# Streaming expert weights on one Trainium2 core: handing over whole 1024-column blocks in place of halves

## The reference

```python
def peer_ffn(h, w_q, sub_keys, expert_u, expert_v):
    ...
    v1, i1 = lax.top_k(s1, PEER_TOPK)
    v2, i2 = lax.top_k(s2, PEER_TOPK)
    cand = (v1[..., :, None] + v2[..., None, :]).reshape(t, PEER_HEADS, PEER_TOPK * PEER_TOPK)
    cs, ci = lax.top_k(cand, PEER_TOPK)
    ...
    gates = jax.nn.softmax(cs, axis=-1)
    def mix(args):
        hc, ec, gc = args
        a = jax.nn.gelu(jnp.einsum('chkd,cd->chk', expert_u[ec], hc).astype(jnp.float32))
        w = (gc * a).astype(hc.dtype)
        return jnp.einsum('chk,chkd->cd', w, expert_v[ec])
```

## Time and profile before

| | us |
|---|---|
| median of 3 executions (3075.44 to 3093.64) | 3091.76 |
| the profiled execution | 3091.76 |
| its span, first to last instruction | 3089.8 |
| TensorE busy in the span | 3043.7 |
| VectorE busy | 2096.0 |
| ScalarE busy | 1603.9 |
| `w_u` stage, from about 789 to 1521 us of the span | 732 |
| `w_v` stage, from 1522 to about 2242 us | 720 |

### The profile page before, as it was taken

How to read it: one execution, slowest core, us unless ns; L and a number is a source line. 1 busy time by engine, 2 the same in 40 slices (tenths; PEclk the granted TensorE clock), 3 DMA queues, 4 the chain that set the end, 5 groups by cost and what they waited for, 6 DMA issues and landing times.

```text
span 3089.8 us, 45798 instructions
## 1 busy us (share of the span) xinstructions
PE 3043.7 (99%) x14773; PEld 2514.2 (81%) x14773; DVE 2096.0 (68%) x4127; ACT 1603.9 (52%) x2955; POOL 480.4 (16%) x341
## 2 busy tenths in 40 slices
PE   7999999999999999999999999999999999999998
PEld 6888787788888888888888888888878888877787
DVE  4567677656888888766666666666576676568864
ACT  4445464455555555555555555555564445546553
POOL 1000000000087867770000000000000000000000
PEclk9999999999999999999999999999999999999999
DMA  6777554466577777886766666666666555653355
GB/s 225 252 256 238 174 159 150 152 189 201 177 190 185 187 188 186 188 185 191 235 209 214 207 214 206 214 227 202 185 190 194 167 177 177 197 170 119 112 157 166
DMA packets 197197, 588.00 MB, mean 190 GB/s; under 512 B 54608, under 2 KB 54736, under 8 KB 195776
## 3 DMA queue, kind: packets, MB, share of 16 engines
q1 hardware_dynamic: 148688, 537.99, 55.8%
q0 software_dynamic: 48368, 48.20, 7.9%
HBM read 565.00 MB, written 21.10 MB: 190 GB/s over the span
## 4 chain that ended last, share of the span: by engine, by line
PE 96%; DVE 2%; DMA 1%; ACT 1%; issue 0%; SPq 0%; POOL 0%; DVEq 0%; ACTq 0%
PE bank L814 17%; PE bank L589 14%; PE bank L591 13%; PE bank L590 13%; PE bank L815 9%; PE bank L884 8%; PE bank L886 8%; PE bank L885 8%; PE bank L654 2%; PE bank L559 1%; PE bank L666 1%; DVE lo L1464 1%; DMA raw<-in_w_narrow 0%; PE bank L677 0%; PE bank L676 0%; DMA raw<-in_w_att 0%
## 5 line engine op out<-in xcount | busy, mean ns | idle before, releaser
L1047 ACT ACTIVATE hi<-raw 128x512 fp32r<-128x512 f32 (+1 forms) x2042 | 1284.7, 632 | 1367.3 <-PE bank L591 640.6
L1464 DVE TENSOR_TENSOR lo<-raw,hi 128x512 fp32r<-128x512 f32 (+1 forms) x2042 | 1388.9, 692 | 843.1 <-ACT hi L1047 826.1
L814 PE MATMUL bank<-xt,hi 128*128 128x512 f32 x2304 | 813.6, 398 | 0.1
L589 PE MATMUL bank<-hi,xt 128*128 128x512 f32 (+1 forms) x1924 | 768.2, 399 | 14.5 <-DVE lo L1464 14.3
L591 PE MATMUL bank<-hi,xt 128*128 128x512 f32 (+1 forms) x1924 | 751.2, 390 | 0.0
L590 PE MATMUL bank<-lo,xt 128*128 128x512 f32 (+1 forms) x1924 | 749.7, 390 | 0.0
L815 PE MATMUL bank<-xt,lo 128*128 128x256 f32 x2304 | 646.5, 281 | 0.0
L814 PEld LDWEIGHTS bank<-xt,hi 128*128 128x128 f32 x2304 | 432.8, 188 | 107.3 <-issue 0.4
L435 POOL DMA_INDIRECT gates_scratch<-picked,place x256 | 420.3, 1642 | 269.2 <-DVE picked L1961 161.4
L589 PEld LDWEIGHTS bank<-hi,xt 128*128 128x128 f32 x1924 | 363.7, 189 | 97.6 <-issue 21.7
L815 PEld LDWEIGHTS bank<-xt,lo 128*128 128x128 f32 x2304 | 435.1, 189 | 0.0
(11 more groups left out here) (215 smaller groups left out, 1598.7 us busy)
## 6 DMA issues: line engine op xcount, KB each, us to landing
raw<-in_w_u SPq DMA_DIRECT2D x256, 512.0 KB
raw<-in_w_v SPq DMA_DIRECT2D x256, 512.0 KB
raw<-in_w_ein SPq DMA_DIRECT2D x128, 512.0 KB
raw<-in_w_oin SPq DMA_DIRECT2D x72, 512.0 KB
raw<-in_w_att SPq DMA_DIRECT2D x64, 512.0 KB
raw<-in_w_gate SPq DMA_DIRECT2D x64, 512.0 KB
gates_scratch<-u_low POOLq DMA_DIRECT2D x16, 1024.0 KB, 7.5
raw<-in_w_out SPq DMA_DIRECT2D x32, 512.0 KB
```

The costliest lines, as they stand in the source:

```text
L589: pe.matmul(acc, xh, h_[:, s], start=first, stop=False)
L814: pe.matmul(acc[:, :], h_[:, s], xt[:, tile].rearrange("p w t -> p (w t)"), start=first, stop=False)
L1047: act.activation(hi[d][:, c], raw[s][:, c], ACT.Copy).then_inc(hi_ready, 2 // parts)
L1464: dve.tensor_tensor(lo[d][:, c], raw[s][:, c], hi[d][:, c].bitcast(F32), ALU.subtract)\
```

## The change

In the two expert stages every split is made with `parts=1`: one ScalarE and one VectorE instruction of 1024 columns in place of two of 512. That covers blocks 1 to 255 of `w_u`, all 256 of `w_v` and the first of `w_ein`. TensorE waits once for a block, ahead of its first matmul, and releases it once, by 2, with its last matmul. In `expert_v` the two inner loops change places: token tile `t` outside, half `n` inside. All other stages keep halves. The number of matmuls and their operands stay as they were.

```diff
@@ expert_u
                 for q in range(2):
                     b = FIRST["w_u"] + 2 * j + q
+                    pe.wait_ge(lo_ready, 2 * (b + 1) if i is None else i * 8 + 2 * (b + 1))
                     h_, l_ = hi[b % 2], lo[b % 2]
                     for kk in range(8):
-                        if kk % 4 == 0:
-                            there = 2 * b + kk // 4 + 1
-                            pe.wait_ge(lo_ready, there if i is None else i * 8 + there)
                         k = 8 * q + kk
                         s = slice(kk * P, kk * P + P)
                         mm = weights_by_tokens(bank[6 + g % 2], h_, l_, s, k, k == 0, k == 15)
-                        if kk % 4 == 3:
-                            mm.then_inc(block_used, 1)
+                    mm.then_inc(block_used, 2)
@@ expert_v
-                    if q == 0:
-                        pe.wait_ge(wlo_ready, j + 1 if i is None else i * 2 + (j + 1))
+                    if i is None:
+                        pe.wait_ge(wlo_ready, j + 1)
+                        pe.wait_ge(lo_ready, 2 * (b + 1))
+                    else:
+                        if q == 0:
+                            pe.wait_ge(wlo_ready, i * 2 + (j + 1))
+                        pe.wait_ge(lo_ready, i * 8 + 2 * (b + 1))
                     h_, l_ = hi[b % 2], lo[b % 2]
-                    for n in range(2):
-                        there = 2 * b + n + 1
-                        pe.wait_ge(lo_ready, there if i is None else i * 8 + there)
-                        if first and q == 1 and n == 0:
+                    for t in range(2):
+                        if first and q == 1 and t == 0:
                             pe.wait_ge(added, N_EXPERT_TILES)
-                        for t in range(2):
-                            wh, wl = w_hi[j % 2][:, t * P:t * P + P], w_lo[j % 2][:, t * P:t * P + P]
+                        wh, wl = w_hi[j % 2][:, t * P:t * P + P], w_lo[j % 2][:, t * P:t * P + P]
+                        for n in range(2):
                             acc = bank[4 * t + 2 * q + n][:, :]
...
-                        mm.then_inc(block_used, 1)
+                    mm.then_inc(block_used, 2)
@@ ScalarE, tile_u (both splits; split_v likewise)
-                split(b, i, 4)
+                split(b, i, 4, parts=1)
@@ VectorE, all splits of the two stages
-                split(FIRST["w_u"] + 1 + b)
+                split(FIRST["w_u"] + 1 + b, parts=1)
...
-                split(b)
+                split(b, parts=1)
```

More of the change, by code:

```diff
@@ L1306, in tile_u @@
                     take_low(j - 1, i)
-                split(b + 1, i, 4)
+                split(b + 1, i, 4, parts=1)
                 if i is None:
@@ L1332, in split_v @@
                 b = FIRST["w_v"] + 2 * j + 1
-                split(b, i, 4 if i is not None else 0)
+                split(b, i, 4 if i is not None else 0, parts=1)
                 if i is not None or j + 1 < N_EXPERT_TILES:
                     high_weights(j + 1, i)
-                split(b + 1, i, 4 if i is not None else 0)
+                split(b + 1, i, 4 if i is not None else 0, parts=1)
             take_low(N_EXPERT_TILES - 1)
@@ L2013, in _ @@
                 for n in range(4):
-                    split(FIRST["w_u"] + 1 + 2 * ROUTE_TILES + n, i, 4)
+                    split(FIRST["w_u"] + 1 + 2 * ROUTE_TILES + n, i, 4, parts=1)
                     if n % 2 == 0:
@@ L2049, in _ @@
                     add_x2(1)
-                split(b + 1)
+                split(b + 1, parts=1)
             def ret_take(h):
```

## The result

The changed kernel took 3106.6 us (median of 9 executions, 3101.93 to 3108.12); the kernel before, on the same chip, 3090.91 us (9 executions). The ratio is 1.0054, with a 95% interval of 1.0041 to 1.0067: 0.5% slower, or 15.7 us. The forecast was 3098 us, in a range from 3078 to 3114. The direction held, and most of the mechanism. The size did not: 6 us were expected on top. The working itself reached only to 3105 us, with the long end of every link; 3106.6 lies in the range because it had been widened for the spread of the executions and for the rivals.

The account below looks back on a forecast made before the run. The prediction took TensorE's own pace to bound both expert stages. It added 5 us of stalls in `w_u` and 1 us at the start of `w_v` to 3091.76 us, giving 3098 us, range 3078 to 3114.

Parts of the forecast that it names:

- What bounds it, and what the change gives: Expert stages: TensorE sets the pace; VectorE saves 84 us and ScalarE 108 us of busy time, worth nothing on the path.
- The lead: Expert-stage handover: lead falls from 2.5 us; next block ready at M + 2.65, wanted at 2.82 or 2.80.
- The stalls in `w_u`: Places where VectorE's other work outlasts the lead and TensorE waits: 4.8 us, called 5, with ends 3 and 11.
- the first Exp: In `w_u`, table load, Exp and four picks make VectorE late by 1.06 us; 0.8 us of it new.
- The nine top-16 stretches: In `w_u`, `add_u` with top-16 steps between two splits: 0.1 us over for each of nine, 0.9 us.
- The six with picks: In `w_u`, `add_u` with four picks between two splits: 0.40 us over for each of six, 2.4 us.
- The budget of 1.77: In `w_u`, VectorE's other work between one block's `lo` and the next may take 1.77 us without stalling TensorE.
- The start of `w_v`: Block 1 late by 0.6 us, later weight loads 0.4 us: 1 us in sum, 0.6 to 2.1.
- the first: Rival: a block's chain exceeds its period, so every block in `w_u` and `w_v` pays; 36 us, 3134 us in all; 7%.
- The clock: Rival: each of 17 stalls brings a stretch at half clock on TensorE, 21 us, 3119 us in all; 3%.
- No change: Rival: the stalls do not show, as VectorE's stretches shrink or the lead grows back; 3092 us; 17%.
- faster: Rival: fewer waits and releases on TensorE save 0.06 us a pair, 31 us, giving 3061 us; 4%.

Follow-up runs that it names:

- `splits_whole`: Changed kernel, but TensorE waits for and releases halves and `expert_v` keeps its old loop order; only the splits are whole: 3104.81 us, ratio 1.0054 to the kernel before.
- `one_count_again`: Changed kernel with the three handover semaphores rising by 1, not 2, per whole block in the expert stages, second timing: 3100.34 us, ratio 1.0040 to the kernel before.
- `one_count_even`: Changed kernel with semaphores rising by 1 per whole block and 14 long routing steps per head pair moved to slots without `add_u`: 3104.08 us, ratio 1.0043.
- `even_before`: Kernel before, with 14 long routing steps per head pair, from the second pair on, moved to slots without `add_u`: 3084.07 us, ratio 0.9981.
- `release_whole`: Kernel before with only TensorE's part of the change (waits, releases, loop order); ScalarE and VectorE split by halves: 3089.07 us, ratio 1.0006.
- `scalar_whole`: Kernel before with only ScalarE's splits whole in the expert stages; VectorE's splits and TensorE's waits and releases stay halves: 3089.61 us, ratio 1.0013.

## Why the prediction was right, and where it was off

- **What bounds it, and what the change gives.** Right. TensorE's pace is what it was, VectorE is busy for 71.6 us less (2096.0 to 2024.4; 84 forecast) and ScalarE for 102.5 us less (108 forecast), and none of it reaches the time. The two durations taken from other lines, 1.219 and 1.053 us, came out at 1.227 and 1.061. That TensorE's waits, releases and loop order are worth nothing on the path is borne out by `splits_whole`, which lacks them and is as slow.
- **The lead.** Right in kind. The step that failed is the pair of handovers in it, "M + 0.20" and "0.03 later". Both were read from halves of `w_v`, whose instructions carry the wait that held them. Whole splits had 0.26 and 0.10, the chain 2.80 us in place of 2.65, and VectorE 1.6 us between two blocks in place of 1.77. The prediction named that end (0.26 and 0.11, 11 us) and did not choose it; while routing even that was short, with 0.28, 0.13 and a chain of 2.85. `w_narrow`, whose splits already raised by 2, had it in the trace of before, and so had ScalarE's halves while routing; I looked at durations of long instructions there and not at their starts.
- **The stalls in `w_u`.** 4.8 forecast, 13.9 measured. Of the 9.1 us between them, 6.3 are the "other" blocks, which the prediction put at nothing. Only 1.6 of the 6.3 lie where VectorE's other work reaches up to the split. In the rest of them VectorE was not late but waiting. Two terms were missing there: the chain, read in `w_v` and taken to fit everywhere, was too long beside the routing, and each late start costs 0.07 us on top of its wait. (The prediction saw such a surplus at the first Exp, 0.26 us lost for a wait of 0.15, and did not carry it over.) By `one_count_again` 4.4 of the 6.3 are the handovers' doing. The nine top-16 stretches were mis-sized by themselves: 0.22 us each even with short handovers, in place of 0.1. The six with picks cost 0.55 in place of 0.40. Their durations were read rightly: in `one_count_again` the gap between the splits of the first of them is 907.99 - 905.78 = 2.21 us. The budget of 1.77 was too wide for the routing: there ScalarE starts 0.10 behind TensorE (M + 0.26) in 159 of 160 waits even in `one_count_again`, as its split carries the wait for the load there and not the one for TensorE, and the splits are 0.01 longer each. That makes 1.69, and 2.21 - 1.69 = 0.52 by it. In the trace of before half of the waits in that stretch had this 0.10; the prediction's row came from `w_v`, where all but a few have 0.04.
- **The start of `w_v`.** 1 us forecast, 1.0 measured. Block 1 lost 0.64 us by its start, as forecast (0.6). The rest lies in small pieces, two of 0.35 us at blocks 82 and 164 among them, whose cause I did not test.
- **The rivals.** The loop closes in the late windows (568 and 429), so the first is out as priced. In the routing part it came true on a small scale: 2.85 us against 2.82 to 2.83. With 0.00 us to spare in `w_v` it was near there too. The clock did not fall: 1.00 behind stalls of 1.04 and 1.28 us. `one_count_even` shows the clock down after a long wait: behind its 19.6 us idle it is at 0.50, that is 1.2 GHz:

```profile
1545.94:1548.50 2.56, 2.56 (x6) 2.08 (x7) 1.10 (x3) 1.67 (x3) 1.05 (x2) 0.50 0.92 333
```

- **No change and faster.** No change is out by the interval, whose lower end is 1.0041. Faster is out by the same interval, and by the spacing of the matmuls, which is the same.
- **Not in the prediction at all:** GpSimd. I took its queue as untouched. It lost half of its slack of 124 us, without a cost in this kernel.

The Trainium skill's rule that spoke against the change ("Perfetto Trace Analysis", Optimizing Scalar/DVE Operations) is what the chip shows here: the coarser instructions freed 72 and 103 us on engines that were not the bound, and cost 15.7 us on the one that was.

No version is shown to be faster than the kernel before, as the ratio of `even_before` rests on its two groups. What the expert stages have left to give is small while TensorE is busy for nearly every microsecond of them; the kernel before is to be kept.

## What to carry to other kernels

Before making handovers coarser, work out the chain of one buffer round (each engine's start, end and handover) against the period of the bounding engine, and then hold each stretch of other work on the feeding engines against the difference. Here about half of the cost came from 17 long stretches that no longer fitted, and most of the rest from blocks where the chain alone was a few hundredths too long, with 0.07 us on top for each late start. Where a chain is tight, let semaphores of coarse steps rise by one, keep the wait that ends last on the instruction itself, and read a handover from an instruction of the very kind, in the very stage, that will be there. And look at queues that only have slack: an engine that seems untouched may have lost half of it.

## What the runs showed of the hardware

- An instruction that carries the wait it was held up by starts sooner than one whose wait stands apart: 0.04 in place of 0.10 us for ScalarE behind TensorE, 0.03 in place of 0.10 for VectorE behind ScalarE. With two waits apart it is mostly 0.12 and 0.13. The wait stands apart where the instruction's own semaphore rises by 2, and also where it rises by 1 but carries another wait (544 of ScalarE's splits in the kernel before). It doesn't matter by how much the sender raised: in `release_whole` TensorE raises by 2, and ScalarE's splits that carry the wait stay at 0.04.
- GpSimd's scatter lasted 1.5 to 2.2 us, most often 1.54, or about 2.5 us. The long ones came only where VectorE ran 1024-column splits: 93 of 256 lasted about 2.5 us or more in the changed kernel, and none over 2.2 us in the kernel before, `scalar_whole` or the three others with VectorE's halves throughout. By the Trainium skill ("SBUF — State Buffer", Who interferes with whom) a VectorE instruction with two inputs in SBUF, as `raw - hi` is, contends with a GpSimd instruction that reads SBUF, and the port they share is locked by one of them at a time. The durations fit that: one instruction of 1.23 us in place of two of 0.69 with a gap between them. No run here tests the port itself.
- TensorE runs the same block of `w_u` in 2.77 or in 2.83 us, at the same granted clock and with no wait: 290 or 285 matmuls in 50 us. It can change within an execution. The kernel before itself runs blocks 7 to 14 at the quick pace, up to the first Exp, where TensorE is late, and all later ones at the other. In the trace of `scalar_whole` it changes behind the first Exp, and behind five of the six blocks with four picks (63, 87, 113, 137 and 163), each time just after TensorE had lost 0.09 us or more. In the kernel before no block after the first Exp was late, and the pace never changed again. The kernel before, over all its executions on record, took 3074.5 to 3080.1 us in 18 of 88 executions and 3087.0 to 3094.0 in the other 70, with nothing between; 256 blocks times 0.055 us are 14 us, so the two groups are probably the two paces, but no trace of an execution of the lower group is there to show it. What picks the pace stays open. None of the 20 executions of the changed kernel and `splits_whole` came below 3101.9. Their chain of 2.80 us or more is longer than a quick block of 2.77, so that a quicker pace would gain them little; this was not tested.
- After a late start TensorE's first pair of matmuls takes longer: 0.42 us in place of 0.35, in 89 of 172 routing blocks of the changed kernel, 51 of `one_count_again`'s and 2 of the kernel before's.
